# Feed-forward multiply-adds laid behind up and down units, and one turn of modulation moved from GpSimd's rkv stage to VectorE's feed-forward

## The chip, the cores and the metric

One Trainium2 chip, of which the program uses one core. The metric is the device time of one execution in microseconds (us), as the median over runs. Inside the profile, times are counted from the start of the span. TensorE has two clock levels, 1.2 and 2.4 GHz; the profile gives the granted clock as a share of the upper one.

## The reference

Two blocks over a sequence of 256 tokens of 2048 features, batch 1, all in float32.

The first block makes a modulation vector `mod = silu(c) @ w_ada + b_ada` of 6 x 2048 numbers (shift, scale and gate of its two halves), then `x = x + gt1 * mixer(norm(x) * (1 + sc1) + sh1)`, where the mixer is an RWKV7 scan over 16 heads next to a pooling mixer, and `x = x + gt2 * ffn(norm(x) * (1 + sc2) + sh2)`, where

```python
u = h @ w_up                       # 2048 x 11264
y = conv_b + sum(conv_w[j] * shifted(u, j) for j in range(3))
val, gate = split(y, 2)
return (silu(gate) * val) @ w_down # 5632 x 2048
```

The second block has a modulation of its own, `silu(c_2) @ w_ada_2` (3 x 2048), a projection to 20032 columns, two attention branches (a latent one and a dilated one) and an output projection. The output is x after both, 256 x 2048.

## The kernel before, in words

**Stages.** In order of time: the "in" stage (first modulation rows and input columns, to about 165 us), the rkv stage (24 units of 128 columns of `w_in`, to 345 us), the wkv stage (the scan, made of small block matmuls, to about 560 us), `w_out` (16 units, to 650 us), the feed-forward (to 1416 us), then the second block (to the end at 2683 us).

**Units.** Nearly all weight traffic goes through a ring of four slots of 1 MB (`ring`). A unit is one such load. SP issues the load (`load`, L448 to L457) once TensorE is through with the unit that had the slot before, four units earlier. ScalarE copies it into a rounded form (`w_high`, L1465), VectorE subtracts to get the rest (`w_low`, L1925), and TensorE multiplies with both. Three products of high and low parts stand for one float32 product. `paired` (L841, L844) does 16 matmuls of 512 columns with `w_high` and then 16 of 256 columns with `w_low`. Both ScalarE and VectorE run up to two units ahead of the unit they evict (`ahead(..., to=2)`).

**The rkv stage.** For every unit VectorE makes `w_low` of the unit two further on, adds the two halves of the result out of PSUM (`added`, L2041), takes the difference to the previous token (`dsh`, L2123) and mixes (L2124); for units 8 to 15 three instructions more make keys (L2139 to L2141). After unit 15 ScalarE squares the keys (L1587), and ahead of unit 18 TensorE sums the squares with 32 matmuls of two columns (L981). Towards the end VectorE makes the factors of the scan: AR (L2109, L2111, L2116), Bt (L2112), the identities X and XT (L2101) and Kt (L2178). The wkv stage begins with products of these (L1052, L1068) and transposes (L1083), with modulation pieces in between (`mod_piece`, L797), whose rows SP loads (`ada_rows`, L469) after the last rkv unit.

**The modulation.** It is made 512 columns at a time, a turn. A turn multiplies 16 tiles of 128 x 512 weights by a column of `silu(c)` each and adds them up; a reduction over the partitions by TensorE (`ada`, L780) then gives four columns of `mod`. Most turns of the first block go through TensorE (`mod_piece`). 17 are done by multiply-adds on other engines:

- two by GpSimd in the rkv stage (`FIRST_TURNS`; the loop L690 to L706): turn 7 of the second block's `w_ada`, then turn 19 of the first's. Each has eight loads of 0.5 MB (`first_turns` on SP, L481 to L490), placed behind rkv units 5 (two), 8, 9, 11, 12, 14, 15, 17, 18, 20, 21, 23 (one each) and three after the last. Per tile GpSimd does a multiply (L699) and an add (L700).
- eleven by VectorE in the feed-forward (`turn_half`, L2368): a turn is four quarters (1 MB each, `ada_quarter`, L471 to L479, two buffers `adf`), a quarter two halves, a half two multiply-adds of 128 x 512 (L2382, L2384, L2386).
- four by GpSimd in the attention.

**The feed-forward.** 11 rounds of 8 up units (128 columns of `w_up`, value and gate in turn) and 4 down units (512 x 512 of `w_down`), the down units of round i behind the up units of round i + 1. In the loop `for i in range(12)` VectorE does for each up unit: `ahead`, every second time `low_hidden`, the convolution (`conv`, L2340 to L2342), every second time `gated`, and then one `turn_half()`, 88 in all from the third up unit of round 0 to the second step of i = 11. Behind the eighth, `down_sums(i - 1)` makes `w_low` and evicts the two banks of each of the four down units, without a half. For i = 11 there are only two short steps, then `down_sums(9)`, whose own `ahead` makes `w_low` of the third and fourth down unit of round 9, and then the last down units with the sums transposed (L1268, L2429).

SP's order is written out by hand: for each round, three quarter loads among the up units and one between the second and third down unit. A quarter load waits until VectorE has freed its buffer (`f_free`), and what stands behind it in SP's queue waits with it. TensorE reduces turn i - 1 after the down units of round i - 1, and VectorE takes its four columns (`ada_take`, L1968).

Of the kernel before, what the change touches and what calls it, by code (L numbers as in the profile page):

```python
# [20 lines left out]
P = 128  # L21
# [119 lines left out]

def last_z_bank(half, i):

    return 2 if (half, i) == (1, 3) else 0
# [5 lines left out]
def program(nc, xT_in, consts, att_consts, params, pos, w_ada, w_in, w2, a2, g2, pool_w, w_out, w_up, w_down,  # L150
            w_ada2, w_in2, w_kvb, w_mla, w_dil, w_o, out):
    ctx = ExitStack()
    with ctx:
# [107 lines left out]
        acc_e = [at(f"acc_e{k}", 8 + 2 * k, [P, 512]) for k in range(2)]  # L261
# [6 lines left out]
        acc2 = [at(f"acc2{b}", W0 + 106 + 2 * b, [P, 512]) for b in range(2)]  # L268
# [112 lines left out]
        N_EARLY, N_FIRST, N_FFN, N_LATE = 8 + 11, 2, 11, 4  # L381
        FIRST_TURNS = ((1, 7), (0, 16 + 3))
# [61 lines left out]
        def _(sp):  # L444
# [115 lines left out]

            ups(0, range(4))
# [3 lines left out]
            ups(0, range(4, 8))  # L565
            quarter(0, 2)
            for i in range(1, 11):
                ups(i, (0, 1))
                if i == 1:
                    quarter(0, 3)  # L570
                ups(i, (2, 3))
                quarter(i, 0)
                ups(i, (4, 5))
                quarter(i, 1)
                ups(i, (6, 7))
                quarter(i, 2)
                downs(i - 1, (0, 1))
                quarter(i, 3)
                downs(i - 1, (2, 3))
# [70 lines left out]
        def _(pool):  # L650
# [39 lines left out]
            for t, (block, _) in enumerate(FIRST_TURNS):  # L690
                for eighth in range(8):
                    pool.wait_ge(f_landed[k % 2], 16 * (k // 2 + 1))
                    for j in range(2):
                        w = AE[k % 2][:, 512 * j:512 * j + 512]
                        col = cact[:, DT * block + 2 * eighth + j:DT * block + 2 * eighth + j + 1]
                        if eighth == j == 0:
                            ins = pool.tensor_scalar(acc_e[t][:, :], w, col, None, ALU.mult)
                        else:
                            after(pool.tensor_scalar(prod_e[:, :], w, col, None, ALU.mult))  # L699
                            ins = pool.tensor_tensor(acc_e[t][:, :], prod_e[:, :], acc_e[t][:, :], ALU.add)  # L700
                        if j == 0:
                            after(ins)
# [58 lines left out]
        def _(pe):  # L761
# [283 lines left out]
            for tt in range(2):  # L1045
# [87 lines left out]
                for c in range(2):  # L1133
# [44 lines left out]
                    if n == 0:  # L1178
                        ada(*acc_e)
# [91 lines left out]
            for i in range(12):  # L1271
# [12 lines left out]
                if i:  # L1284
# [4 lines left out]
                    ada(acc2[(i - 1) % 2])  # L1289
# [168 lines left out]
        def _(act):  # L1458
# [242 lines left out]
            for s in range(4):  # L1701
                if s == 1:
                    act.wait_ge(f_free, 8 * N_FIRST + 4 * N_FFN)
# [208 lines left out]
        def _(v):  # L1912
# [278 lines left out]
            for tt in range(2):  # L2191
# [33 lines left out]
                for c in range(2):  # L2225
# [15 lines left out]
                    if n == 0:  # L2241
                        v.wait_ge(ada_full, AFTER + 1)
                        v.tensor_copy(mod[:, 76:80], bank[6][:, 4:8])
                        v.tensor_tensor(mod[:, 124:128], bank[6][:, 0:4], pr("b_ada", 124, 4), ALU.add).then_inc(ada_free, 1)
# [123 lines left out]
            def turn_half():  # L2368

                h = B.up("turn_half") - 1  # L2370
                if h < 0 or h >= 8 * N_FFN:
                    return
# [4 lines left out]
                acc = acc2[turn % 2][:, :]  # L2377
# [13 lines left out]
            B.n["turn_half"] = -2  # L2391

            def down_sums(r):
                for s in range(4):
                    ahead("down", r, s)
                    unit("down", r, s)
                    for m, o in ((0, bank[s]), (1, bank[down_bank(r, s)])):
# [4 lines left out]
                        else:  # L2402
                            evicted(r, s, m, v.tensor_copy(d, u))
                ada_take(5 * DT + 4 * r)

            for i in range(12):
                for n in range(8):
                    if i < 11:
                        ahead("up", i, n)
                    if n % 2 and (n > 1 or i):  # L2410
# [7 lines left out]
                    turn_half()  # L2418
# [41 lines left out]
            ada_take(5 * DT + 40)  # L2460
# [334 lines left out]
```

## Time and profile before

| what | us |
|---|---|
| median of 3 runs (2675.55, 2683.62, 2675.67) | 2675.67 |
| the profiled execution's own time | 2684.82 |
| its span | 2683.0 |
| TensorE matmul busy | 2586.4 (96%) |
| VectorE busy | 1885.0 (70%) |
| ScalarE busy | 1099.5 (41%) |
| GpSimd busy | 472.3 (18%) |

The span runs from the first to the last instruction, the execution's own time has 1.8 us around it. The mean granted clock is 0.975. The main DMA queue takes 72.0% of the span of the 16 DMA engines, and all move 213 GB/s. A ring load of `w_up` takes 5.8 us from issue to landing. In a timeline, a line is start, duration, engine, source line and operation, xcount, and in brackets the idle time before it with what ended it. Matmuls overlap, so one's duration is more than its share; their starts are the measure. A stretch (from:to) has its length, then the busy time of PE, PEld, DVE, ACT and POOL with their instructions, PEclk, the DMA share and GB/s; of an engine alone, only that one's.

### The profile page before, as it was taken

To read this page: it belongs to the slowest core of one execution; us is meant where nothing else is said; L and a number is where in the kernel's file an instruction comes from. 1 tells how busy PE (TensorE), PEld (TensorE's weight loads), DVE (VectorE), ACT (ScalarE), POOL (GpSimd) and SP (SyncE) were. 2 spreads that over 40 slices of the span, in tenths; PEclk is the share of its full clock that TensorE was granted. 3 is DMA by queue.
4 is the path that set the end of the run, shared out by engine and by line. 5 is a ranking of instruction groups with operands and counts; after the bars stand their busy time and mean duration, and the time that the engine had idled before them with its cause. 6 is when DMAs were issued, how large, how long until landed. Compare 5 with 4: busy or idle time off the path is not lost.

```text
span 2683.0 us, 41988 instructions
## 1 busy us (share of the span) xinstructions
PE 2586.4 (96%) x18000; PEld 2243.8 (84%) x18000; DVE 1885.0 (70%) x2453; ACT 1099.5 (41%) x1312; POOL 472.3 (18%) x304
## 2 busy tenths in 40 slices
PE   6999989999999999999999999999999999999997
PEld 3678767788878888888889999999888888889996
DVE  2249863277899999999986778676547874886554
ACT  2243322144444444444455454454434443444453
POOL 0057641012000000000001576770000000000001
PEclk8899889899999999999999999999999999999998
DMA  9968557776988888888855886885766656666664
GB/s 338 339 169 235 165 199 252 241 228 173 247 249 250 250 251 250 250 250 251 250 196 134 210 225 214 220 218 163 191 195 175 173 167 180 176 168 173 188 184 115
DMA packets 744985, 570.21 MB, mean 213 GB/s; under 512 B 44608, under 2 KB 629440, under 8 KB 744672
## 3 DMA queue, kind: packets, MB, share of 16 engines
q1 hardware_dynamic: 744800, 567.52, 72.0%
q8 instruction: 143, 2.34, 0.4%
q14 instruction: 42, 0.34, 0.0%
HBM read 565.38 MB, written 2.10 MB: 212 GB/s over the span
## 4 chain that ended last, share of the span: by engine, by line
PE 81%; DVE 13%; DMA 2%; issue 2%; POOL 1%; ACT 1%; SPq 0%; DVEq 0%; POOLq 0%
PE bank L841 29%; PE bank L844 15%; PE bank L808 4%; PE bank L809 3%; PE bank L810 3%; DVE w_low L1925 3%; PE bank L1246 3%; PE bank L1248 3%; PE bank L1247 3%; PE bank L1094 2%; PE bank L797 2%; PE bank L879 2%; PE bank L877 2%; PE bank L878 2%; PE bank L1143 1%
## 5 line engine op out<-in xcount | busy, mean ns | idle before, releaser
L1925 DVE TENSOR_TENSOR w_low<-ring,w_high 128x2048 fp32r<-128x2048 f32 (+1 forms) x389 | 894.0, 2300 | 317.2 <-ACT w_high L1465 310.6
L841 PE MATMUL bank<-acts,w_high 128*128 128x512 f32 x4128 | 993.9, 393 | 3.4 <-ACT w_high L1465 1.8
L1465 ACT ACTIVATE w_high<-ring 128x2048 fp32r<-128x2048 f32 (+1 forms) x389 | 738.2, 1900 | 375.6 <-DMA ring<-w_up 137.7
L841 PEld LDWEIGHTS bank<-acts,w_high 128*128 128x128 f32 x4128 | 760.1, 189 | 154.7 <-issue 2.8
L844 PEld LDWEIGHTS bank<-acts,w_low 128*128 128x128 f32 x4128 | 528.9, 191 | 24.5 <-DVE w_low L1925 4.8
L844 PE MATMUL bank<-acts,w_low 128*128 128x256 f32 x4128 | 535.9, 283 | 2.9 <-DVE w_low L1925 2.9
L667 POOL TENSOR_TENSOR sumf<-sqf 128x256 f32<-128x256 f32 x1 | 0.7, 743 | 781.2 <-ACT sqf L1906 781.2
L731 POOL TENSOR_TENSOR sumy<-sqy 128x256 f32<-128x256 f32 x1 | 2.1, 2094 | 760.7 <-ACT sqy L1722 760.7
L745 POOL TENSOR_SCALAR prod_g<-adg,cact 128x512 f32<-128x512 f32 x60 | 121.1, 2018 | 66.9 <-DMA adg<-w_ada 63.6
L1246 PE MATMUL bank<-w_high,hid_high 128*128 128x512 f32 x320 | 126.1, 394 | 6.6 <-DVE w_low L1925 6.6
L1248 PE MATMUL bank<-w_high,hid_low 128*128 128x512 f32 x320 | 125.9, 394 | 0.0
L1247 PE MATMUL bank<-w_low,hid_high 128*128 128x512 f32 x320 | 125.8, 393 | 0.0
L749 POOL TENSOR_TENSOR acc_g<-prod_g,acc_g 128x512 f32<-128x512 f32 x60 | 111.5, 1858 | 5.0
L797 PE MATMUL bank<-ada,c_wide 128*32 128x512 f32 x608 | 92.4, 699 | 20.0 <-DMA ada<-w_ada 17.9
L808 PE MATMUL bank<-mix_high,w_high 128*128 128x256 f32 x384 | 108.8, 283 | 0.0
L810 PE MATMUL bank<-mix_high,w_low 128*128 128x256 f32 x384 | 108.7, 283 | 0.0
L809 PE MATMUL bank<-mix_low,w_high 128*128 128x256 f32 x384 | 108.7, 283 | 0.0
L808 PE MATMUL bank<-acts,w_high 128*128 128x256 f32 (+2 forms) x288 | 87.8, 305 | 14.7 <-DVE acts L2006 8.5
L2384 DVE SCALAR_TENSOR_TENSOR acc<-adf,cact,acc 128x512 f32<-128x512 f32 x121 | 90.7, 750 | 3.1
L809 PE MATMUL bank<-acts,w_high 128*128 128x256 f32 (+2 forms) x288 | 85.3, 296 | 0.0
L810 PE MATMUL bank<-acts,w_low 128*128 128x256 f32 (+2 forms) x288 | 84.9, 295 | 0.0
L1684 ACT ACTIVATE rawu<-bank 128x256 f32<-128x256 f32 x88 | 33.5, 381 | 118.7 <-PE bank L844 116.7
(471 smaller groups left out, 3615.6 us busy)
## 6 DMA issues: line engine op xcount, KB each, us to landing
ring<-w_in SPq DMA_DIRECT2D x176, 1024.0 KB, 5.8
ring<-w_up SPq DMA_DIRECT2D x88, 1024.0 KB, 5.8
ada<-w_ada SPq DMA_DIRECT2D x76, 1024.0 KB, 6.3
adf<-w_ada SPq DMA_DIRECT2D x44, 1024.0 KB, 5.2
ring<-w_down SPq DMA_DIRECT2D x44, 1024.0 KB, 7.4
ring<-w_out SPq DMA_DIRECT2D x16, 1024.0 KB, 5.9
adg<-w_ada SPq DMA_DIRECT2D x64, 256.0 KB, 5.5
ring<-w_mla SPq DMA_DIRECT2D x16, 1024.0 KB, 5.7
```

The source lines that it names most:

```text
L745: pool.tensor_scalar(o, AG[k % 2][:, :].rearrange("p (a b) -> p a b", a=2), cact[:, DT + j:DT + j + 1], None, ALU.mult).then_inc(g_free, 1)
L797: mm = pe.matmul(bank[6][32 * j:32 * j + 32, :], CB[home(t)][:, 4 * q + j, :], AD[q][:, 512 * j:512 * j + 512], start=q == 0, stop=q == 3, ...
L808: pe.matmul(o, wh, ah, start=first, stop=False, skip_group_check=True)
L809: pe.matmul(o, wh, al, start=False, stop=False, skip_group_check=True)
L810: return pe.matmul(o, wl, ah, start=False, stop=last, skip_group_check=True)
L841: pe.matmul(o, wh[:, j], both, start=j == 0, stop=False, skip_group_check=True)
L844: mm = pe.matmul(o[:, 0:T], wl[:, j], AH[:, j, :], start=False, stop=j == 15, skip_group_check=True)
L1246: pe.matmul(o[:, :], hh, wh[:, j], start=j == 0, stop=False, skip_group_check=True)
L1247: pe.matmul(o[:, :], hh, wl[:, j], start=False, stop=False, skip_group_check=True)
L1248: mm = pe.matmul(o[:, :], hl, wh[:, j], start=False, stop=j == 3, skip_group_check=True)
L1465: act.activation(WH[s][:, 0:WIDE[n]], ring[s][:, 0:WIDE[n]], ACT.Copy).then_inc(high_done, 1)
L1925: v.tensor_tensor(WL[s][:, 0:WIDE[n]], ring[s][:, 0:WIDE[n]], f32(WH[s][:, 0:WIDE[n]]), ALU.subtract)\
```

## The change

GpSimd makes one turn in the rkv stage and not two (`N_FIRST` 1, `FIRST_TURNS` only turn 19 of the first block). The other becomes the twelfth turn of the feed-forward (`N_TURNS` 12), and its reduction goes with that of turn 10, in one take of eight columns. The 96 halves are laid out by a table: `halves_behind(i)` gives the up units and the down units of pass i that have a half behind them, 5 in pass 0, 4 + 4 in pass 1, 6 + 4 in passes 2 to 4, 5 + 4 in passes 5 to 9, 5 + 0 in pass 10 and 3 down in pass 11. `quarter_loads()` puts quarter k behind the ring load that stands four units after half 2k - 3. In pass 11 ScalarE and VectorE make the high and low part of the third and fourth down unit of round 9 in the two short steps ahead of the sums. There are three accumulators in place of two.

```diff
+def halves_behind(i):
+    ups = {0: (2, 4, 5, 6, 7), 1: (1, 3, 5, 7), 10: (1, 3, 5, 6, 7)}.get(i, (1, 2, 3, 5, 6, 7) if i < 5 else (1, 3, 5, 6, 7))
+    return ups, (0, 1, 2, 3) if 0 < i < 10 else (0, 1, 2) if i == 11 else ()
+
+def quarter_loads():
+    order, halves = [], []
+    for i in range(12):
+        ups, downs = halves_behind(i)
+        for n in range(8 if i < 11 else 0):
+            order.append(("up", i, n))
+            halves += [len(order) - 1] * (n in ups)
+        if i:
+            order += [("down", i - 1, s) for s in range(4)]
+        halves += [len(order) - 4 + s for s in (downs if i < 10 else halves_behind(11)[1] if i == 10 else ())]
+    behind = {}
+    for k in range(2, len(halves) // 2):
+        behind.setdefault(order[halves[2 * k - 3] + 4], []).append(k)
+    return behind
...
-        N_EARLY, N_FIRST, N_FFN, N_LATE = 8 + 11, 2, 11, 4
-        FIRST_TURNS = ((1, 7), (0, 16 + 3))
+        N_EARLY, N_FIRST, N_TURNS, N_FFN, N_LATE = 8 + 11, 1, 12, 11, 4
+        FIRST_TURNS = ((0, 16 + 3),)
...
-                elif k in (8, 9, 11, 12, 14, 15, 17, 18, 20, 21, 23):
+                elif k in (8, 9, 11, 12, 14, 15):
                     first_turns(1)
-            first_turns(3)
...
             quarter(0, 0)
             quarter(0, 1)
-            ups(0, range(4, 8))
-            quarter(0, 2)
+            for k in range(4, 8):
+                ups(0, (k,))
+                behind("up", 0, k)
             for i in range(1, 11):
...
+                for k in range(8):
+                    ups(i, (k,))
+                    behind("up", i, k)
+                for s in range(4):
+                    downs(i - 1, (s,))
+                    behind("down", i - 1, s)
...
                     if n == 0:
-                        ada(*acc_e)
+                        ada(acc_e)
...
-                    ada(acc2[(i - 1) % 2])
+                    ada(*[acc2[t % 3] for t in ((i - 1,) if i < 11 else (10, 11))])
...
                     if i < 11:
                         ahead(UNIT["up", i, k] + 2)
+                    else:
+                        ahead(UNIT["down", 9, k] + 2)
...
             def down_sums(r):
...
+                    if s in halves_behind(r + 1 if r < 9 else 11)[1]:
+                        turn_half()
                 ada_take(5 * DT + 4 * r)
...
                     if i < 11:
                         ahead("up", i, n)
+                    else:
+                        ahead("down", 9, n)
...
-                    turn_half()
+                    if i < 11 and n in halves_behind(i)[0]:
+                        turn_half()
...
-            ada_take(5 * DT + 40)
+            ada_take(5 * DT + 40, 8)
```

## Rows read from the trace of the kernel before

**Rows 1.** One feed-forward round: the stretch, then VectorE's groups in it

```profile
1226.00:1293.40 67.40, 67.40 (x363) 58.41 (x363) 61.08 (x79) 28.47 (x28) 0.00 (x0) 1.00 0.82 251
...
L2384 DVE SCALAR_TENSOR_TENSOR acc<-adf,cact,acc 128x512 f32<-128x512 f32 x11 | 8.2, 750 | 0.3
...
L2401 DVE TENSOR_TENSOR dacc<-bank,dacc 128x512 f32<-128x512 f32 x8 | 5.1, 685 | 0.9 <-PE bank L1248 0.9
```

**Rows 2.** Waits of TensorE from 680 to 1340 us, then from 1340 to 1500

```profile
PE bank L1246 <- DVE w_low L1925: 3.2, 1, 3.2
...
PE bank L841 <- ACT w_high L1465: 1.8, 2, 1.6
...
PE bank L1246 <- DVE w_low L1925: 3.4, 1, 3.4
```

**Rows 3.** Stretches behind two of them: busy by engine, PEclk, DMA share, GB/s

```profile
755.00:760.00 5.00, 5.00 (x17) 3.96 (x16) 4.86 (x7) 1.30 (x3) 0.00 (x0) 0.70 1.05 397
...
1375.00:1380.00 5.00, 4.60 (x13) 3.69 (x14) 5.00 (x7) 3.31 (x4) 0.00 (x0) 0.66 0.31 118
```

**Rows 4.** VectorE's timeline in the rkv stage

```profile
271.71 1.06 DVE L2123 TENSOR_TENSOR dsh<-raw 128x256 f32<-128x256 f32 x1
...
276.43 2.66 DVE L1925 TENSOR_TENSOR w_low<-ring,w_high 128x2048 fp32r<-128x2048 f32 x1
...
293.15 0.43 DVE L2123 TENSOR_TENSOR dsh<-raw 128x256 f32<-128x256 f32 x1
...
295.93 2.29 DVE L1925 TENSOR_TENSOR w_low<-ring,w_high 128x2048 fp32r<-128x2048 f32 x1
```

**Rows 5.** GpSimd's timeline in the same stage

```profile
275.64 0.10 POOL L706 MEMSET small<- 128x1 f32 x1
...
294.93 1.56 POOL L699 TENSOR_SCALAR prod_e<-ade,cact 128x512 f32<-128x512 f32 x1 [5.27 <-DMA ade<-w_ada]
...
372.90 2.35 POOL L710 TENSOR_TENSOR rk<-rkv 128x1024 f32<-128x1024 f32 x1 [13.69 <-DVE small L2210]
```

**Rows 6.** TensorE's timeline in the same stage

```profile
292.84 2.17 PE L844 MATMUL bank<-acts,w_low 128*128 128x256 f32 x16 [1.53 <-DVE w_low L1925]
...
298.10 6.96 PE L981 MATMUL bank<-con,kksq 128*128 128x2 f32 x32 [3.10 <-ACT kksq L1587]
...
304.93 6.64 PE L841 MATMUL bank<-acts,w_high 128*128 128x512 f32 x16
```

**Rows 7.** A stretch of TensorE alone: busy, PEclk, DMA share, GB/s

```profile
300.00:305.00 5.00, 5.00 (x25) 0.50 0.28 98
```

**Rows 8.** VectorE's timeline at the stage's end; L2101 by itself, min/median/max ns

```profile
335.83 3.27 DVE L1925 TENSOR_TENSOR w_low<-ring,w_high 128x2048 fp32r<-128x2048 f32 x1
...
341.73 1.16 DVE L2111 TENSOR_SCALAR AR<-kk 128x16 f32<-128x16 f32 x1
...
347.42 1.04 DVE L2123 TENSOR_TENSOR dsh<-raw 128x256 f32<-128x256 f32 x1
...
359.22 2.29 DVE L2178 TENSOR_TENSOR Kt<-rkv,exq 128x2048 f32<-128x2048 f32 x1
...
L2101 DVE COPY X<-cmask x4: 419/635/1487, 354.6 to 448.3; 128x512 f32<-128x512 f32 x4
```

**Rows 9.** TensorE's timeline at the first transposes

```profile
361.56 0.73 PE L1083 MATMUL bank<-con,Bt 128*128 128x128 f32 x4 [2.06 <-DVE Kt L2178]
```

**Rows 10.** SP's issues after the last rkv unit, and their landing

```profile
345.20 39.25 SPq L469 DMA_DIRECT2D ada<-w_ada  x10
...
DMA to landing us min/median/max: 5.0/7.5/13.0
```

**Rows 11.** TensorE's timeline at the last reduction of the feed-forward

```profile
1415.92 0.95 PE L780 MATMUL bank<-con,acc 128*128 128x1 f32 x8
```

**Rows 12.** SP's waits for VectorE from 735 to 760 us, then one round

```profile
SPq L479 <- DVE acc L2386: 17.9, 2, 10.8
...
SPq L479 <- DVE acc L2386: 16.4, 3, 6.5
```

More of the change, by code:

```diff
@@ L139 @@
 TURN_BANK = (5, 7, 4, 7)
+def halves_behind(i):
[15 more added lines that the diff above has]
+    return behind
+QUARTERS = quarter_loads()
 def last_z_bank(half, i):
@@ L260, in program @@
         AE = [at(f"ade{k}", 4 * k, [P, 1024]) for k in range(2)]
-        acc_e = [at(f"acc_e{k}", 8 + 2 * k, [P, 512]) for k in range(2)]
+        acc_e = at("acc_e", 8, [P, 512])
         prod_e = at("prod_e", 12, [P, 512])
@@ L267, in program @@
         ROW = [at(f"mod_row{k}", W0 + place, [P, 512]) for k, place in enumerate((109.75, 109))]
-        acc2 = [at(f"acc2{b}", W0 + 106 + 2 * b, [P, 512]) for b in range(2)]
+        acc2 = [at(f"acc2{b}", W0 + place, [P, 512]) for b, place in enumerate((106, 108, 104))]
         BH = at("mix_high", W0 + 32, [P, 8, T], F32R)
@@ L559, in quarter, with behind @@
                 ada_quarter(w, first, q)
+            def behind(*key):
+                for k in QUARTERS.get(key, ()):
+                    quarter(k // 4, k % 4)
             ups(0, range(4))
@@ L564, in _ @@
             quarter(0, 1)
-            ups(0, range(4, 8))
-            quarter(0, 2)
+            for k in range(4, 8):
+                ups(0, (k,))
+                behind("up", 0, k)
             for i in range(1, 11):
[L568 to L579, printed above, removed]
+                for k in range(8):
[4 more added lines that the diff above has]
+                    behind("down", i - 1, s)
             downs(10, range(4))
@@ L696, in _ @@
                         if eighth == j == 0:
-                            ins = pool.tensor_scalar(acc_e[t][:, :], w, col, None, ALU.mult)
+                            ins = pool.tensor_scalar(acc_e[:, :], w, col, None, ALU.mult)
                         else:
                             after(pool.tensor_scalar(prod_e[:, :], w, col, None, ALU.mult))
-                            ins = pool.tensor_tensor(acc_e[t][:, :], prod_e[:, :], acc_e[t][:, :], ALU.add)
+                            ins = pool.tensor_tensor(acc_e[:, :], prod_e[:, :], acc_e[:, :], ALU.add)
                         if j == 0:
@@ L1702, in _ @@
                 if s == 1:
-                    act.wait_ge(f_free, 8 * N_FIRST + 4 * N_FFN)
+                    act.wait_ge(f_free, 8 * N_FIRST + 4 * N_TURNS)
                     from_dve()
@@ L2242, in _ @@
                         v.wait_ge(ada_full, AFTER + 1)
-                        v.tensor_copy(mod[:, 76:80], bank[6][:, 4:8])
-                        v.tensor_tensor(mod[:, 124:128], bank[6][:, 0:4], pr("b_ada", 124, 4), ALU.add).then_inc(ada_free, 1)
+                        v.tensor_copy(mod[:, 76:80], bank[6][:, 0:4]).then_inc(ada_free, 1)
             act_moved(1, "U", 1, 0)
@@ L2376, in turn_half @@
                     v.wait_ge(f_landed[k % 2], 16 * (k // 2 + 1))
-                acc = acc2[turn % 2][:, :]
+                acc = acc2[turn % 3][:, :]
                 for j in (2 * m, 2 * m + 1):
@@ L2389, in turn_half @@
                     v.memset(small[:, 56:57], 0.0).then_inc(ada_sums, 1)
-            B.n["turn_half"] = -2
             def down_sums(r):
```

2 lines of the change are left out of this document (removed).

## The prediction, made before the change was run

> **What bounds the kernel now.** I read the waits of TensorE by stage first, then the stretches with the granted clock, then the three engines' timelines where a stage shows waits. In the steady feed-forward part TensorE is busy for the whole of an iteration (67.4 of 67.4 us) while VectorE is busy for 61.1 of it [rows 1]: VectorE's load there costs nothing until it outruns TensorE. In all of the feed-forward stage TensorE waits at three places only, 3.2 us and 1.8 us around the first down units and 3.4 us before the third down unit of the last round [rows 2], and behind each long wait it runs a while at a lower granted clock (0.70 and 0.66 of full over 5 us, so part of it at the lower level of 1.2 GHz) [rows 3].
>
> The other place is the rkv stage. There the chain that ended last runs through VectorE, not TensorE, from about 212 us to 296 us and again from 334 us to 361 us. What the reader is to see is one instruction at two prices: the shift difference takes 1.06 us at 271.71 and 0.43 us at 293.15 [rows 4]. GpSimd is at work at the first and waits 5.27 us for a load at the second. It has its first turn done at 275.64, works on its second from 276 to 359, and has nothing to do after that until 372.90 [rows 5].
>
> **What the change removes in the rkv stage: A, the middle.** GpSimd's second turn goes: 8 loads of 0.5 MB on SP's queue, 31 arithmetic instructions on GpSimd. Turn (0, 19) now comes first and keeps the time of the old first one, so up to 275.6 nothing changes. From 276.43 to 295.93 VectorE does three units in 19.5 us, 6.5 each; the third, with GpSimd waiting for nearly all of it, is 5.44 with one instruction still slowed. Without that one, a unit is w_low 2.20 (start to start), 0.45 and 0.46, 0.52, 0.38, 0.47 and 0.52, together 5.0 [rows 4]. Three make 15.0, so the last key is ready at 291.4 and not 295.9: 4.5 us. TensorE stood for that key: it finished its matmuls at 295.0, waited 3.10 us and began the 32 two-column sums at 298.10 [rows 6]. In the new order it finishes at 291.9 and waits until 293.7, and the sums start 4.4 us earlier. The small waits before (1.53 us at 292.84) are inside this figure, not beside it.
>
> The clock is the open term. The sums and the unit behind them run at a granted clock of 0.50 [rows 7], the lower of its two levels, after that wait: 6.96 us of sums, and 6.64 us for 16 wide matmuls [rows 6] that take 3.8 elsewhere. If the clock stays up, up to 6.2 us more are gained (2.8 on the unit and some 3.4 on the sums, taken at half). If it falls all the same, nothing. The wait becomes shorter (1.8 for 3.1), but the sums behind it are tiny. I take 2.5.
>
> **B, the end of the rkv stage.** From 329 us VectorE works without a gap up to Kt at 359.22. Instructions slowed beside GpSimd: w_low 3.27 for 2.29; a 16-element TENSOR_SCALAR at 1.16, with its like at 0.56 (1.4 too much at most, 0 at least, since no undisturbed one is shown); a dsh at 1.04 and what follows it, 0.9; the last rkv, 0.9; four copies of 4.6 us in all, against 0.42 each at their shortest, 2.8 [rows 8]. Sum 5.6 to 7.0 us. TensorE waited for Kt until 361.56 [rows 9]. But what is late next is a load: SP sends the modulation rows of this stage only when the last rkv unit is done, at 345.20, and the quickest takes 5.0 us to land [rows 10]. So the first modulation piece can't start before 350.2. With the piece (1.9), the products (3.7 at the lower clock, 1.9 at the full) and the next piece (1.2) the transposes start at 355 to 357, 4.6 to 6.5 us earlier. I take 5.5. The two missing 0.5 MB loads at 343 can only bring that load forward.
>
> Here the Trainium skill (SBUF — State Buffer, Who interferes with whom) has a sharper rule: an instruction of VectorE with two SBUF inputs and a GpSimd instruction that reads SBUF shut each other out for the whole instruction. By that, each of the 18 such steps in A would wait half a GpSimd instruction of 1.6 us, some 14 us instead of 4.5. The rows say 0.6 us where one is held up, and many are not held up at all; I stay with the rows.
>
> **C1, first feed-forward rounds.** Before, VectorE does a half (two multiply-adds of 0.75 us, 1.56 with gaps [rows 1]) behind every up unit. Two up units take it 12.25 us, 6.1 each, against 5.57 of TensorE; without the half it is 4.57. So it falls 0.55 us behind per up unit and catches up in the down units, where it has 3.4 (w_low 2.2, two evictions 1.2 [rows 1]) against 5.45. Before the first down unit 16 up units stand in a row, with 14 halves: hence the 3.2 us wait for w_low. After, 9 halves stand there, 7.8 us less work, and the wait goes, with the clock loss behind it (0.30 of 5 us, 1.5). The 1.8 us of waits for w_high come from a ring load that SP sent late, since it stood behind a quarter load that waited 10.8 us for VectorE; with VectorE early that goes too. Sum 6.5 us, at worst 3 [rows 2, 3, 12].
>
> **C2, last round.** w_low of the third and fourth down unit was made only inside the sums of round 9, behind the last two halves. Now both ScalarE and VectorE make them two steps earlier, and the halves there are gone. Of 3.4 + 1.7 us (clock 0.66 over 5 us) I keep 4.5: the fourth down unit's load stands behind quarter 47 in SP's queue and may hold VectorE some 2 us, of which about 1 reaches the transposed sums. Between 3.5 and 5.1.
>
> **What the change adds, at nothing.** The twelfth turn: 8 halves, 12.5 us of VectorE, and 4 loads of 1 MB. The fullest rounds (2 to 4) have 10 halves: up 8 x 4.57 + 6 x 1.56 = 45.9 us against 44.6, down 4 x (3.4 + 1.56) = 19.8 against 21.8 and a 0.9 us reduction. Together 65.8 of 67.3: hidden, with 1.5 us a round to spare; were that cover gone, each half would cost its 1.56. The DMA share goes from 0.82 [rows 1] to some 0.87. A ring load goes out when a unit ends, takes 5.8 us to land (the DMA issues) and 1.9 us of ScalarE, and is wanted 16.7 us later: 9 us of slack. A column reduction of 8 matmuls (0.95 us) leaves the wkv stage and comes back at 1415.92 [rows 11], where TensorE is not waiting: net nothing. The third accumulator and the wider take (8 columns for 4) cost no instruction more.
>
> **Sum.** 4.4 + 2.5 + 5.5 + 6.5 + 4.5 = 23.4 us. Against the profiled execution's 2684.8 that is 2661.4. The median of the runs is 9.1 us below it: two runs at 2675.6, one at 2683.6. Where these 9 us lie I can't see. If they lie outside the places named, the median falls to 2652.3; if they are partly a clock loss counted above, it falls less. I give back a little: **2654**.
>
> **Rivals.**
> 1. Both sites pay (above): 0.60, 2646 to 2662.
> 2. Only one pays: the rkv gain is taken back by the modulation rows, which SP can't send earlier (feed-forward alone, 11.0 us: 2665), or the new positions bring other waits into the feed-forward and only the 12.4 us of A and B stay (2663). For it: the load floor in B. Against it: TensorE waits for no modulation row anywhere between 350 and 530 us. 0.24.
> 3. Next to nothing, because the 9 us are the same thing that is removed, or the clock falls at new places: 2668 to 2676. 0.11.
> 4. Slower: SP's queue. Each quarter load waits for a half of VectorE, before 3 times a round, up to 6.5 us [rows 12], and every ring load behind it waits too. Now there are up to five a round and halves stand behind evictions. If a quarter holds up its ring load by more than the 9 us of slack, TensorE waits in every round. It decides from 0.55 us a quarter, which over 44 quarters eats all 23.4; at 1 us it gives 2696. Against it: the wait is for a half of the unit that has just ended, some 5 us. 0.05. That the change does not do what it says I can rule out from the diff: 96 halves and 48 quarters are laid out.
>
> **Numbers.** A measurement of this kernel tells about 0.3% (8.0 us) from no change; faster means below 2667.6. Cases 1 and 2 are faster: 0.84. Case 3: same, 0.11. Case 4: slower, 0.05. The range for 8 in 10 takes in case 1 with the clock term at its top (2644) and case 2, up to 2668.
>
> **What would show it.** GpSimd idle from 276 us; dsh at 0.42 from there on; the two-column sums at about 293.7, and if their unit takes 5.6 us and not 8.4, the clock term is at its top; the transposes at some 352 on the new time axis (A and B together 12 us earlier); no wait over 1 us of TensorE in rounds 0 to 10; VectorE at 0.97 of rounds 2 to 4. Wrong: a wait of TensorE for w_high or w_low in every round, or the wkv stage starting earlier and ending at the old time.

## The result, and the profile after

The changed kernel takes 2660.72 us (median of 4 runs, 2658.12 to 2664.16) against 2679.64 (median of 4) for the kernel before on the same chip: a ratio of 0.9922, 95% interval 0.9901 to 0.9944. So it is faster by 0.56 to 0.99%, and inside the range of 2644 to 2668. In the medians the gain is 18.9 us, where the forecast had 21.7 (2675.67 to 2654). Its profiled execution took 2664.16 us with a span of 2662.3, that of before 2684.82 with 2683.0: 20.7 us, where the sum of the forecast was 23.4.

The sum is best checked by places. The table gives the first start, on TensorE, of work that both kernels do (the timeline of each), and how much earlier it is after the change.

| start of | before, us | after, us | earlier by |
|---|---|---|---|
| two-column sums of kksq | 298.10 | 294.11 | 4.0 |
| (end of the last rkv matmul) | 345.17 | 340.02 | 5.2 |
| transposes behind Kt | 361.56 | 350.87 | 10.7 |
| w_out | 559.15 | 543.58 | 15.6 |
| first down unit | 753.97 | 734.15 | 19.8 |
| first transposed sum (matmul 1 of 32) | 1388.84 | 1364.58 | 24.3 |
| last transposed sum (matmul 32 of 32) | 1398.53 | 1377.75 | 20.8 |
| sums of sqy | 1416.73 | 1396.84 | 19.9 |
| (end of the span) | 2683.0 | 2662.3 | 20.7 |

VectorE in the rkv stage, the lines that answer to [rows 4] (timeline; start us, us):

```profile
272.18 1.06 DVE L2149 TENSOR_TENSOR dsh<-raw 128x256 f32<-128x256 f32 x1
...
276.90 2.29 DVE L1951 TENSOR_TENSOR w_low<-ring,w_high 128x2048 fp32r<-128x2048 f32 x1
279.56 0.42 DVE L2149 TENSOR_TENSOR dsh<-raw 128x256 f32<-128x256 f32 x1
...
281.91 2.29 DVE L1951 TENSOR_TENSOR w_low<-ring,w_high 128x2048 fp32r<-128x2048 f32 x1
```

GpSimd, to [rows 5]:

```profile
276.12 0.10 POOL L730 MEMSET small<- 128x1 f32 x1
359.45 2.35 POOL L734 TENSOR_TENSOR rk<-rkv 128x1024 f32<-128x1024 f32 x1 [83.24 <-DVE small L2236]
```

From the moment GpSimd stops, a unit of VectorE takes 5.01 us (w_low at 276.90 and at 281.91), where 5.0 was worked out. TensorE, to [rows 6] and [rows 9] (timeline), and its stretches, to [rows 7]:

```profile
294.11 6.11 PE L1005 MATMUL bank<-con,kksq 128*128 128x2 f32 x32 [1.56 <-ACT kksq L1611]
...
341.77 1.16 PE L1076 MATMUL bank<-Bt,AR 64*64 64x64 f32 x64 [1.74 <-issue]
345.36 1.11 PE L821 MATMUL bank<-ada,c_wide 128*32 128x512 f32 x8 [2.43 <-DMA ada<-w_ada]
...
350.87 1.09 PE L1107 MATMUL bank<-con,Bt 128*128 128x128 f32 x8
```

```profile
295.00:300.00 5.00, 5.00 (x26) 0.51 0.58 156
300.00:305.00 5.00, 5.00 (x14) 0.50 0.01 3
```

The wait for kksq is 1.56 us for 3.10, but the clock falls behind it all the same, to 0.51 and 0.50: the lower of its two levels for nearly 10 us. The wait for Kt is gone, and what is late now is the load of the modulation rows (2.43 us).

Waits of TensorE in the feed-forward stage, 640 to 1320 us and then 1320 to 1420, to [rows 2] (us in total, times, longest):

```profile
PE bank L1270 <- DVE w_low L1951: 2.9, 5, 1.6
...
PE bank L1292 <- DVE dacc L2422: 1.3, 1, 1.3
PE bank L832 <- DVE xT L2455: 0.8, 1, 0.8
```

The 3.2 and 3.4 us before the down units and the 1.8 us for w_high are gone. A wait of 1.6 us for the same w_low is left at the first down unit (the forecast had none over 1 us in rounds 0 to 10), and two new ones stand behind the last units. Where these are, in the timeline of TensorE and in the stretch behind them:

```profile
1364.58 1.95 PE L1292 MATMUL bank<-con,dacc 128*128 128x128 f32 x16
1367.81 1.06 PE L1292 MATMUL bank<-con,dacc 128*128 128x128 f32 x8 [1.28 <-DVE dacc L2422]
1369.68 0.35 PE L832 MATMUL bank<-hid_high,w_high 128*128 128x256 f32 x1 [0.81 <-DVE xT L2455]
...
1395.13 1.84 PE L804 MATMUL bank<-con,acc 128*128 128x1 f32 x16
1396.84 1.97 PE L1317 MATMUL bank<-sqy,con 128*128 128x256 f32 x8
```

```profile
1370.00:1375.00 5.00, 5.00 (x32) 5.00 (x31) 4.76 (x8) 1.35 (x1) 0.00 (x0) 0.66 0.00 0
```

Two rounds of the feed-forward, of which the first is the fuller one, to [rows 1] (busy PE, PEld, DVE, ACT, POOL, then PEclk, DMA share, GB/s), and SP's waits for VectorE in the fullest, to [rows 12]:

```profile
870.00:937.00 67.00, 66.24 (x348) 56.50 (x348) 63.48 (x83) 28.02 (x29) 0.00 (x0) 1.00 0.90 264
...
1213.00:1280.00 67.00, 67.00 (x361) 58.07 (x360) 62.44 (x81) 28.46 (x29) 0.00 (x0) 1.00 0.87 258
```

```profile
SPq L505 <- DVE acc L2409: 35.7, 5, 9.1
```

SP now waits 35.7 us of a full round for VectorE, twice what it did, and no ring load comes too late for TensorE by it: behind the first down unit its only waits in the rounds are four of 0.4 us at most, 1.3 us together. The rival with SP's queue did not come about there.

### The profile page after: what moved, and what is told of

Its sections match the earlier page's. It is cut to its first block, busy times and chain, and to the rows that moved or that the text cites. A ratio compares the mean times of both kernels' runs of the same rounds, so it can differ in the third digit from the quotient of the medians.

```text
span 2662.3 us, 41991 instructions
## 1 busy us (share of the span) xinstructions
PE 2578.9 (97%) x18000; PEld 2238.7 (84%) x18000; DVE 1877.7 (71%) x2469; ACT 1097.0 (41%) x1312; POOL 413.3 (16%) x272
## 4 chain that ended last, share of the span: by engine, by line
PE 78%; DVE 13%; DMA 4%; issue 2%; ACT 2%; POOL 1%; SPq 0%; DVEq 0%; POOLq 0%
PE bank L865 28%; PE bank L868 14%; PE bank L832 4%; DVE w_low L1951 4%; PE bank L833 3%; PE bank L834 3%; PE bank L1118 2%; PE bank L821 2%; PE bank L1270 2%; PE bank L1271 2%; PE bank L1272 2%; DMA ring<-w_up 2%; PE bank L903 2%; PE bank L902 2%; PE bank L901 2%
## 5 line engine op out<-in xcount | busy, mean ns | idle before, releaser
L2407 DVE SCALAR_TENSOR_TENSOR acc<-adf,cact,acc 128x512 f32<-128x512 f32 x132 | 98.9, 749 | 3.0
L832 PEld LDWEIGHTS bank<-acts,w_high 128*128 128x128 f32 (+2 forms) x288 | 57.3, 199 | 25.7 <-issue 14.0
```

The source lines that it names most:

```text
L832: pe.matmul(o, wh, ah, start=first, stop=False, skip_group_check=True)
```

## The experiments

The ratios are against the kernel before on the same chip, with their 95% intervals; "start" and "end" are of the profiled execution, on the axis of the table above. Four kernels ran on one chip, four on a second and three on a third; the kernel before had 2679.65, 2678.62 and 2678.61 us there.

### 1. Only the arithmetic of the second GpSimd turn, and the turn as a whole

```diff
-                    for j in range(2):
+                    for j in range(2 if t == 0 else 0):
```

This is the kernel before with all 16 loads for GpSimd kept and the arithmetic of the second one left out (so what goes through this turn is not computed). In the second kernel its loads are gone too:

```diff
-        N_EARLY, N_FIRST, N_FFN, N_LATE = 8 + 11, 2, 11, 4
+        N_EARLY, N_FIRST, N_FFN, N_LATE = 8 + 11, 1, 11, 4
...
-                for eighth in range(8):
+                for eighth in range(0 if t else 8):
```

> The kernel before, but GpSimd does no arithmetic for its second turn: the eight loads of 0.5 MB and their waits on SP's queue stay, each is answered by a one-column memset. Left out: turn 19 of the first block (four columns of mod hold turn 7's sums instead). Theory S (VectorE was slowed by GpSimd working beside it): the whole gain of the first stages comes without taking away a load, TensorE reaches the first wide matmul of w_out at about 544 us (559 before) and the span is 2683 - 15 = 2668. Theory L (the loads between the rkv loads, and the last one ahead of the modulation rows, were what cost): nearly nothing, w_out at 557 to 559, span 2681 to 2683.

> The kernel before with GpSimd's second turn left out whole, loads and arithmetic; the feed-forward is untouched. Left out: turn 19 of the first block. Both theories: w_out begins at about 544 us. Theory S: same as the run with the loads kept, within 1.5 us. Theory L: 12 us or more earlier than that run. In either case the feed-forward keeps its 3.2 us and 3.4 us waits, and the span is 2667 to 2669.

Measured: 2666.83 us, 0.9956 (0.9940 to 0.9972) without the arithmetic, and 2667.18 us, 0.9956 (0.9940 to 0.9973) without the loads as well. In the profiles the transposes start at 349.3 and 348.8 us for 361.6 before, and w_out at 536.8 and 537.9 for 559.1. The dsh of VectorE, without the arithmetic (timeline):

```profile
280.75 1.07 DVE L2125 TENSOR_TENSOR dsh<-raw 128x256 f32<-128x256 f32 x1
...
286.40 0.42 DVE L2125 TENSOR_TENSOR dsh<-raw 128x256 f32<-128x256 f32 x1
```

GpSimd's last addition ends at 281.5 us there. What follows: the gain in the rkv stage comes from GpSimd's arithmetic beside VectorE; 8 loads of 0.5 MB more or less on the queue move nothing that a measurement tells. About 12 us of the median come from this half of the change. Both profiles are the fastest executions of their kernels, 4 to 8 us under the medians, so their ends (2657.3 and 2661.6) overstate it, as do the starts of w_out, which the expectation had at 544: what comes on top is the clock of the wkv stage (experiment 7).

### 2. Only the layout of the multiply-adds

The kernel with the new positions, but with both GpSimd turns and eleven in the feed-forward; then the same without the second GpSimd turn, which is the change less its twelfth turn (the columns of the turn left out are then not computed):

```diff
-    ups = {...}.get(i, (1, 2, 3, 5, 6, 7) if i < 5 else (1, 3, 5, 6, 7))
+    ups = {...}.get(i, (1, 3, 5, 6, 7) if i < 5 else (1, 3, 5, 7))
...
-        N_EARLY, N_FIRST, N_TURNS, N_FFN, N_LATE = 8 + 11, 1, 12, 11, 4
+        N_EARLY, N_FIRST, N_TURNS, N_FFN, N_LATE = 8 + 11, 2, 11, 11, 4
```

> GpSimd keeps both turns in the rkv stage; only the feed-forward is laid out anew, with 88 halves (5 + 4 in passes 2 to 4 and 4 + 4 in passes 5 to 9, one up half fewer than in the changed kernel; passes 0, 1, 10 and 11 as there). Theory R (the new layout gains 4 to 5 us at the first down units and as much at w_low of the last round, and gives the latter back because three halves stand among the last evictions): start of w_out unchanged at 559, first down unit 4 us earlier, transposed sums 8 us earlier, second block 4 to 5 us earlier, span about 2678. Rival: the gain at the last round is kept and the span is 2674; or the layout alone gains nothing, 2683.

> The changed kernel without the twelfth turn: one turn on GpSimd, the new layout with 88 halves. Left out: turn 7 of the second block. If the two parts are independent, its gain is the sum of the run without the second turn and the run with the layout alone, 15 + 4.5: span about 2663. If the twelfth turn costs nothing, as forecast, it equals the changed kernel (2662.3) within 1.5 us, less the 0.9 us of its reduction. If the extra halves cost in rounds 2 to 9 (1.6 us of small waits there in the changed kernel), it is 2 to 3 us faster, 2660.

Measured: the layout alone 2672.55 us, 0.9969 (0.9955 to 0.9982); without the second GpSimd turn 2654.96 us, 0.9909 (0.9884 to 0.9934). Of the waits before the down units, this is left in the layout alone (TensorE, 640 to 1320 us):

```profile
PE bank L1271 <- DVE w_low L1952: 0.7, 1, 0.7
```

The parts multiply within the noise: 0.9956 x 0.9969 = 0.9925, and 0.9909 was measured with eleven turns, 0.9922 with twelve. In this profile the rkv stage is that of before (last rkv matmul to the transposes 16.4 us, with the wait of 2.15 us for Kt), and from the feed-forward's first matmul (655.24 before, behind a wait for `acts`) to the first down unit it takes 93.6 us for 98.7 before. So the first rounds are worth 5.2 us here, 4.5 in the second kernel and 4.3 in the change itself. Its last round has the two new waits, 1.6 and 0.8 us, so these come with the layout. The twelfth turn costs nothing that the times tell, since the intervals of 0.9909 and 0.9922 overlap. The profiles do show something: from the first down unit to the first transposed sum it takes 628.0 and 627.9 us in these two kernels with eleven turns, and 628.5 to 630.4 in the six profiles with twelve that keep the positions of the change (before: 634.9).

### 3. No multiply-adds in the last round

```diff
-    ... (1, 2, 3, 5, 6, 7) if i < 5 else (1, 3, 5, 6, 7))
-    return ups, (0, 1, 2, 3) if 0 < i < 10 else (0, 1, 2) if i == 11 else ()
+    ... (1, 2, 3, 5, 6, 7) if i < 8 else (1, 3, 5, 6, 7))
+    return ups, (0, 1, 2, 3) if 0 < i < 10 else ()
```

> The changed kernel with no multiply-adds behind the down units of the last round: its three are put behind one more up unit each of rounds 5, 6 and 7, and a fourth accumulator holds the turn that this carries over. Theory G (three multiply-adds of 1.07 us, set among the evictions of the last down units, delay the transposed sums, which TensorE then waits for at a lowered clock): the waits of 1.3 us for the sums and 0.8 us for their transposes go; from the first to the last transposed sum it takes 9.7 us as before, in place of 13.2; the sqy sums start 3 to 4 us sooner than after the change (1396.8), less up to 1.5 us for the heavier rounds 5 to 7, so at 1393 to 1395.5, with the end at 2658 to 2660 in its profile and a ratio of 0.991 (0.989 to 0.993). Rival H (the give-back is the work of the down units and the clock themselves, and would be there without them): first to last transposed sum still takes 12.5 us or more, and the three rounds that get one more multiply-add each lose 1 us each: sqy at 1397 to 1399, ratio 0.992 to 0.9935.

Measured: 2657.82 us, 0.9922 (0.9905 to 0.9940). What the expectation calls three multiply-adds are three halves of two each (0.75 us each). TensorE's timeline at the transposed sums:

```profile
1362.77 0.58 PE L804 MATMUL bank<-con,acc 128*128 128x1 f32 x4
1363.21 2.82 PE L1292 MATMUL bank<-con,dacc 128*128 128x128 f32 x24
1366.31 0.36 PE L832 MATMUL bank<-hid_high,w_high 128*128 128x256 f32 x1 [0.28 <-DVE xT L2455]
```

First to last transposed sum takes 9.7 us for 13.2, and 9.7 again with both edits in experiment 4: theory G holds, and the cause of the give-back is shown. But from the first down unit to the first transposed sum it takes 632.0 us (631.6 with both edits) for 630.4, the price of three fuller rounds, and the net, some 2 us, is less than the measurement tells. This version is not better.

### 4. The token sums one unit later, and both edits together

```diff
-                elif k == 18:
+                elif k == 19:
                     o = x_bank(5)
```

> The changed kernel with the 32 narrow kksq token-sum matmuls (128x2 each) issued one unit later, so that TensorE doesn't wait 1.56 us for them. Theory W (the wait ahead of the sums lowers the clock to 0.51): no wait of over 0.3 us there, the granted clock stays at 1.00 through 290 to 305 and the three units after it take 5.0 us each; sums and units are through 3 to 4 us sooner. Rival N (the narrow sums themselves, 6 us with little work in the array, lower the clock): the wait goes but the clock falls all the same, and only the 1.6 us come back. In either case the transposes at 350.9 rest on loads that were issued by the SP queue, so that theory L (the loads bind there) says they move by under 1 us and the wait for ada, 2.4 us now, grows by what was gained; if the loads are not what binds, the transposes and everything after them come 1.5 to 4 us sooner. I expect N and L: ratio 0.992, as the changed kernel, within 0.0015.

> Both edits together: no multiply-adds in the last round, and the kksq sums one unit later. Nothing is left out: it would be the better version. If G holds and N and L hold, it is the first edit's gain alone: ratio 0.991 (0.989 to 0.993), sqy sums at 1393 to 1395.5. If W holds and loads don't bind, another 3 to 4 us: ratio 0.9895.

Measured: 2653.20 us, 0.9905 (0.9885 to 0.9926), and 2654.53 us, 0.9911 (0.9891 to 0.9932). The sums in the first of them, which now wait for nothing, and then the stretch behind them (all engines, as above):

```profile
296.43 2.08 PE L868 MATMUL bank<-acts,w_low 128*128 128x256 f32 x16
298.35 4.00 PE L1005 MATMUL bank<-con,kksq 128*128 128x2 f32 x32
```

```profile
300.00:305.00 5.00, 5.00 (x25) 4.42 (x25) 4.83 (x8) 2.02 (x3) 0.00 (x0) 0.64 0.73 199
305.00:310.00 5.00, 5.00 (x22) 4.17 (x21) 2.72 (x4) 0.00 (x0) 0.00 (x0) 0.67 0.00 0
```

The wait is gone and the clock falls all the same, as rival N has it. The transposes start at 347.8, 1.4 us before those of the unaltered kernel in experiment 7; that is within what two profiles of one kernel differ by (350.9 and 349.2). The expectation on the load was wrong in one point: the wait for it stayed 2.4 us, since SP sends it when the last rkv unit is done, and it moves with that unit.

### 5. What the turn that GpSimd still makes costs

```diff
-                    for j in range(2):
+                    for j in range(2 if eighth == 0 else 0):
```

The arithmetic of the remaining GpSimd turn is left out but for its first eighth, the loads stay.

> The changed kernel with the arithmetic of the one turn that GpSimd still makes (216 to 276 us) left out but for its first eighth; the loads stay. Theory P (TensorE itself paces 216 to 276 us: it is busy 10.00 of every 10 us and never waits for VectorE there, though VectorE is at 0.97): VectorE's dsh falls from 1.08 to 0.42 us and its busy share to about 0.85, but the units of TensorE keep their pace, and at 276 us all stand within 1 us of the changed kernel; the gain is 0 to 1 us. Rival V (VectorE paces it, with TensorE's pipelined records hiding it): 8 dsh at 0.65 us and one w_low at 0.9 us are 6.1 us, and the unit that starts at 276.9 on VectorE starts 4 to 6 us sooner. Behind it the loads of theory L may still hold the transposes. I expect P at 60 to 40: ratio 0.991 to 0.992 under P, 0.990 under V.

Measured: 2651.95 us, 0.9905 (0.9885 to 0.9925). TensorE's timeline:

```profile
290.86 3.63 PE L1007 MATMUL bank<-con,kksq 128*128 128x2 f32 x32
294.35 3.92 PE L867 MATMUL bank<-acts,w_high 128*128 128x512 f32 x16
...
333.61 1.16 PE L1078 MATMUL bank<-Bt,AR 64*64 64x64 f32 x64 [1.74 <-issue]
337.25 1.94 PE L823 MATMUL bank<-ada,c_wide 128*32 128x512 f32 x8 [2.49 <-DMA ada<-w_ada]
```

Up to 276 us theory P is right: the unit that starts at 274.88 on TensorE after the change starts at 274.16 here. But VectorE is then ahead, so that TensorE waits neither for w_low nor for kksq, the 32 sums take 3.63 us for 6.11 and the clock stays at 1.00 throughout 290 to 310. The transposes start at 342.6 us, 8.3 earlier than after the change and 6.6 earlier than in the profile of experiment 7. The ratio doesn't tell it from the change's (0.9922 and 0.9903), so that whether a place for this turn elsewhere would pay stays open.

### 6. Which of GpSimd's instructions hold VectorE up

```diff
+                            if eighth == 0:
+                                after(pool.tensor_scalar(prod_e[:, :], w, col, None, ALU.mult))
-                            after(pool.tensor_scalar(prod_e[:, :], w, col, None, ALU.mult))
                             ins = pool.tensor_tensor(acc_e[:, :], prod_e[:, :], acc_e[:, :], ALU.add)
```

This one leaves out the scalings behind the first eighth; the second one keeps them and leaves out the additions.

> GpSimd's remaining turn (216 to 276 us) with its scalings (128x512, 24.3 us in all) left out behind the first eighth, its additions (31.8 us) and the loads kept. Leaving out both brought the transposes from 350.9 to 342.6 us. Theory T (VectorE's tensor_tensor stretches whenever GpSimd works at all): about half of that comes back, by the share of the busy time that is left: VectorE's 9 dsh of this stretch are a mix of 0.43 and 1.07 us, transposes at 346 to 348, end in its profile at 2652 to 2657. Rival A (the two-input additions are what collides): nearly all dsh still take 1.07, transposes at 349 to 351, end at 2659 to 2663.

> The reverse: the scalings kept, the additions left out behind the first eighth. Theory T: 43% of GpSimd's busy time is left, so a little over half of the gain: transposes at 345.5 to 348, end at 2651 to 2656, dsh a mix. Rival A: dsh at 0.43 throughout but for the first eighth, transposes at 342.5 to 344.5, end at 2645 to 2650.

Measured: 2652.93 us, 0.9908 (0.9891 to 0.9925), and 2654.01 us, 0.9907 (0.9891 to 0.9924); transposes at 349.3 and 348.5 us. GpSimd and then VectorE with the additions alone (timelines):

```profile
264.83 2.92 POOL L725 TENSOR_TENSOR acc_e<-prod_e,acc_e 128x512 f32<-128x512 f32 x2 [9.56 <-DMA ade<-w_ada]
...
265.54 1.07 DVE L2150 TENSOR_TENSOR dsh<-raw 128x256 f32<-128x256 f32 x1
266.64 1.39 DVE L2151 SCALAR_TENSOR_TENSOR rkv<-dsh,par,raw 128x256 f32<-128x256 f32 x1
268.07 0.35 DVE L2166 TENSOR_SCALAR kk<-rkv,par 128x256 f32<-128x256 f32 x1
268.45 0.42 DVE L2167 SCALAR_TENSOR_TENSOR ktmp<-aa,rkv 128x256 f32<-128x256 f32 x1
```

and with the scalings alone:

```profile
263.48 3.48 POOL L723 TENSOR_SCALAR prod_e<-ade,cact 128x512 f32<-128x512 f32 x2 [8.50 <-DMA ade<-w_ada]
...
263.52 0.42 DVE L2151 TENSOR_TENSOR dsh<-raw 128x256 f32<-128x256 f32 x1
263.98 0.71 DVE L2152 SCALAR_TENSOR_TENSOR rkv<-dsh,par,raw 128x256 f32<-128x256 f32 x1
264.73 0.71 DVE L2167 TENSOR_SCALAR kk<-rkv,par 128x256 f32<-128x256 f32 x1
265.47 0.88 DVE L2168 SCALAR_TENSOR_TENSOR ktmp<-aa,rkv 128x256 f32<-128x256 f32 x1
```

Undisturbed, the four take 0.42, 0.48, 0.35 and 0.42 us. Two additions (2.92 us) cost VectorE 0.65 + 0.91 = 1.56 us; two scalings (3.48 us) 0.23 + 0.36 + 0.46 = 1.05 us. Together that is 2.6 us, and with both a unit of VectorE is 7.38 us (269.52 to 276.90) for 5.01, 2.4 more. So both kinds hold it up, the additions some more: theory T, though dsh itself is not the mix that either theory expected. In time neither half brings anything against the unaltered kernel (0.9903), which fits VectorE's being hidden behind TensorE up to 276. Theory T's transposes (346 to 348 and 345.5 to 348) were missed, and with both left out they came at 342.6. Why the halves don't add up to that stays open: these two profiles started their third rkv unit at 205.7 and 204.8 us, that of experiment 5 at 200.4.

The lines also show how long a held instruction waits. The two additions end at 267.75, and the second held instruction 0.28 us later, at 268.03. In the profile with the additions alone each of the 12 held-up instructions of VectorE between 200 and 300 us ends 0.2 to 0.4 us behind an addition, so it waited for the rest of the addition in progress. The two scalings end at 266.96, and the instruction held beside the second one 0.6 us before that, at 266.35.

### 7. The changed kernel once more

> The changed kernel once more, unaltered, on this chip and beside these two. The profiles so far differ by up to 6 us in when TensorE starts its first rkv units (189.8 to 195.6), for kernels that are the same up to there. Theory O (that lag is absorbed by the stretch that VectorE paces, so it brings no wait at 276 and a higher clock behind the sums): if this profile starts at 189 to 190, it has the waits of 0.5 us and 1.6 us and its transposes come at 350 to 351.5; if it starts at 193 to 196, it has neither wait and the transposes come at 351 to 353. Ratio 0.992 (0.990 to 0.994) in either case.

Measured: 2651.61 us (5 of 6 runs at 2649.7 to 2651.8, one at 2659.3), 0.9903 (0.9887 to 0.9918). The profile started its rkv units at 189.9, had the 1.57 us wait for kksq and the transposes at 349.2, a little before the expected 350. But from the transposes to w_out it takes 183.9 us, and in the first profile of the same kernel 192.7. TensorE alone, first the profile of the result, then this one (busy, PEclk, DMA share, GB/s):

```profile
490.00:510.00 20.00, 20.00 (x290) 0.67 0.65 211
510.00:530.00 20.00, 20.00 (x150) 0.67 1.07 322
```

```profile
490.00:510.00 20.00, 20.00 (x335) 0.79 1.04 350
510.00:530.00 20.00, 19.11 (x155) 0.79 0.82 260
```

The granted clock is 0.67 in one and 0.79 in the other, in a stage that the change doesn't touch but for eight small matmuls. Taken over the 200 us behind the transposes, one minus the clock adds up to 18.8 us in the first and 10.2 in the second. Of all profiles of the kernels with one GpSimd turn or less, five have 18.7 to 18.8 there and six 10.2 to 13.8. This is the size of the gap in the times of this kernel (2651.8 to 2659.3) and of the one with eleven turns in experiment 2 (2650.7 to 2659.2).

## Why the prediction was right, and where it was not

**A, the middle of the rkv stage**, forecast 4.4 and 2.5 for the clock. The sums start 4.0 us earlier, though GpSimd's first turn ended 0.5 us later in this profile: the term is right, and so is its cause (experiment 1). The clock term is not: the last rkv matmul ends only 5.2 us earlier, so the clock brought 1.2. The step that failed is "I take 2.5", of at most 6.2: the sums took 6.11 us for 6.96 and the wide matmuls behind them 6.34 for 6.64. The wait ahead doesn't decide it: of the eight profiles without any wait before the sums the clock fell in seven (experiments 1 to 4 and 6) and stayed in one (experiment 5).

**B, the end of the stage**, forecast 5.5. From the last rkv matmul to the transposes it takes 10.85 us for 16.39 [rows 9]: 5.5. In all eleven profiles without the second turn's arithmetic it is 10.6 to 12.1, in both with it 16.4. The floor by SP's load is there: 5.3 us from the last matmul to the first modulation piece, 5.4 in experiment 5 where all was 8 us earlier, with the wait of 2.43 us that the forecast had as "what is late next". (Its 4.6 to 6.5 us should read 4.6 to 6.4, by its own terms.)

The sentence on the Trainium skill (SBUF — State Buffer, Who interferes with whom) was rightly left out of the sum: 14 us by the forecast's reckoning from it in A, 4.0 measured. But it is the reckoning, 18 steps of half an instruction each, that is off. Beside additions the traces agree with the rule: a held instruction ends 0.28 us behind the addition (experiment 6; before the change ktmp ends at 275.87 and the addition at 275.58). Beside scalings they don't: it ends 0.6 us before the scaling does. In the unit of 7.38 us four instructions of VectorE are held, by 0.3 to 1.05 us each, 2.4 us in all, and the others go at full speed; the forecast's 0.6 us is dsh alone. Experiment 6 adds that a one-input scaling on VectorE (kk, 0.35 to 0.71 us) is stretched too, which the same section allows for scalings in their two-port modes.

**The wkv stage**, forecast nothing beyond the transposes. It brought 4.9 us, the largest gain that was not seen. In the profile of before, the wait of 2.06 us for Kt [rows 9] is followed by one of 0.8 us for X and by 10 us at a clock of 0.66, while after the change the 10 us behind the transposes run at 1.00 (TensorE alone, before and after):

```profile
361.50:371.50 10.00, 9.14 (x100) 0.66 0.35 113
```

```profile
350.80:360.80 10.00, 9.46 (x174) 1.00 1.06 385
```

The reduction of acc_e starts 15.0 us earlier, 4.3 more than the transposes:

```profile
431.75 1.92 PE L780 MATMUL bank<-con,acc_e 128*128 128x1 f32 x16 [0.35 <-ACT mod L1494]
```

```profile
416.78 1.02 PE L804 MATMUL bank<-con,acc_e 128*128 128x1 f32 x8 [0.35 <-ACT mod L1518]
```

From the transposes to it, the two profiles with the second turn's arithmetic take 70.2 and 68.4 us and the eleven without it 64.6 to 66.4, so this part holds beyond one pair of profiles. The reduction itself is 8 matmuls for 16, another 0.9 us. Up to w_out 0.3 us are lost again, in a part that differs by 7 us between executions of one kernel (experiment 7). The step that failed is that B's account ended where the transposes start: the lateness of VectorE, and the clock behind it, went on behind them.

**C1, the first rounds**, forecast 6.5 with 3 at worst, came to 4.3. The waits of 3.2 and 1.8 us are gone as argued, but "the wait goes" was too much: 1.6 us of it stay at the first down unit (1.4 with eleven turns, 0.7 with the layout alone). SP and then ScalarE ahead of it:

```profile
710.15 0.37 SPq L505 DMA_DIRECT2D adf<-w_ada  x1
710.56 4.52 SPq L483 DMA_DIRECT2D ring<-w_up  x2
```

```profile
723.66 1.92 ACT L1489 ACTIVATE w_high<-ring 128x2048 fp32r<-128x2048 f32 x1 [2.38 <-DMA ring<-w_up]
```

SP waited 8.4 us for VectorE before the quarter load at 710.15, and two ring loads went out right behind it. ScalarE waited 2.38 us for the second of them, and VectorE, which by then had no backlog, 0.21 us for ScalarE. It then evicted a unit and did one more half (1.5 us) before it began the w_low that TensorE waits for. So what is left hangs on the queue and on that half, and not on a backlog of VectorE as the forecast counted it; no run tells the two apart.

**C2, the last round**, forecast 4.5. The first transposed sum is 4.4 us closer, and then 3.5 of it are given back. The failing step is "of which about 1 reaches the transposed sums": the cause was looked for in a late load, and it is the three halves themselves, set among the last evictions, with 1.28 and 0.81 us of waits and the clock at 0.66 behind them. Experiment 3 shows it: without them the give-back is gone. Its size depends on the clock: it is 3.5 to 3.9 us in the three profiles where the clock falls there (the change, and the two of experiment 2), and 1.8 to 2.2 in the five with the same positions where it stays at 1.00, that of experiment 7 among them.

**The twelfth turn at nothing**: nearly right for the rounds, where it costs 0.5 to 2.5 us in all (experiment 2), with 63.5 us of VectorE in a round of 67 (0.95, forecast 0.97). But "where TensorE is not waiting: net nothing" for the reduction was two errors in one. Eight more matmuls on a busy engine cost their 0.9 us (1.84 for 0.95 [rows 11]); it is net nothing only because the wkv stage gained the same.

**Sum**: 4.0 + 1.2 + 5.5 + 4.9 + 4.3 + 4.4 - 3.5 - 0.9 + 0.8 = 20.7, as measured. The 0.8 lies behind the sqy sums, where the profiles take 1264.7 to 1266.9 us without any order: scatter. Terms that were 8.4 us too high and gains of 5.7 us that were not seen offset each other in part, so that the sum came out closer than its terms is luck. Of the rivals, the slower one with SP's queue and the one with the load floor in B are excluded by the rows above, and "next to nothing" by the interval; "both sites pay" is shown by experiments 1 and 2, of which each is faster alone.

**The median.** The 9 us by which the profile of before lay above its median were left open. Experiment 7 shows a spread of the same size in one kernel, between an execution at 0.67 and one at 0.79 in 490 to 530 us. That it is the same in the kernel before was not seen, as all its profiles are of one execution.

## What to carry to other kernels

Read where a late engine's lateness ends, not only the first wait that it causes: behind the wait for Kt came one for X and 10 us at a lower clock, and the stage behind the wait gained 4.9 us of its own. A second engine's arithmetic can slow the engine beside it that sets the pace (here 7.38 us a unit for 5.01); moved to a stage where its new host has slack, it cost at most 3.4 us in these profiles. And put such filler work nowhere near the last evictions of a stage, where nothing is left to hide it: three halves took back 1.8 to 3.9 us, of some 4 to 7 gained.

## What the runs showed of the hardware that was not expected

**The granted clock of one stage of small matmuls differs between executions of the same kernel**, 0.67 against 0.79 over 40 us, and 8.8 us of time with it (183.9 for 192.7 from the transposes to w_out). A single profile can't show a gain of 5 us in such a kernel; two of the same kernel ended at 2662.3 and 2647.9 us.

**A late start is absorbed.** TensorE started its first rkv units anywhere from 188.8 to 195.6 us, in kernels that are the same up to there. Of the ten profiles with one turn's arithmetic on GpSimd or half of it, five were late by their third unit (204.8 to 209.1 us for some 201). They waited neither for w_low nor for kksq, and reached the transposes at 348.5 to 352.8, the five others at 347.8 to 350.9.

**The clock behind narrow sums.** In stretches of 5 us from 295 to 310 us, during and behind the 32 two-column matmuls, the lowest granted clock was 0.50 in four profiles (before, the layout alone, the change, both edits of experiment 4), 0.64 to 0.78 in eight and 1.00 in one. TensorE had waited 3.1, 3.7, 1.6 and 0 us before the sums in the four, and up to 1.6 us in the eight, six of which had no wait at all. So the wait alone doesn't decide it, and what does was not found.
